# Gate and up products of a SwiGLU feed-forward as seven block products, the feed-forward in four straight-line parts with a ring of eight weight operands

## The reference

```python
D_MODEL, D_FF = 1024, 2816
def rmsnorm(x, g):
    return x * lax.rsqrt(jnp.mean(x * x, axis=-1, keepdims=True) + EPS) * g
def swiglu(h, w_gate, w_up, w_down):
    return (jax.nn.silu(h @ w_gate) * (h @ w_up)) @ w_down
def trunk(x, ...):
    for i in range(2):
        x = x + 0.5 * rmsnorm(swiglu(rmsnorm(x, ng[0]), gate[i, 0], up[i, 0], down[i, 0]), ng[1])
        h = rmsnorm(x, ng[2])
        y = pool_mixer(h) if i == 0 else gated_deltanet(h)
        x = x + rmsnorm(y, ng[3])
        x = x + 0.5 * rmsnorm(swiglu(rmsnorm(x, ng[4]), gate[i, 1], up[i, 1], down[i, 1]), ng[5])
```

## Time and profile before

| | us |
|---|---|
| median of three runs | 2585.25 |
| the profiled execution | 2587.87 |
| its span, first to last instruction | 2586.1 |
| TensorE matmul busy | 2445.6 |
| VectorE busy | 1290.9 |
| ScalarE busy | 872.7 |
| GpSimd busy | 233.9 |
| mean granted TensorE clock | 0.973 |

### The profile page before, as it was taken

One profiled execution on the slowest core, in us unless ns is written; L12 is line 12 of the kernel. 1 busy time (PEld: TensorE's weight loads), 2 busy tenths in 40 slices (PEclk: granted clock), 3 DMA queues, 4 the chain that ended last, 5 costly groups with the idle time before them and its releaser, 6 DMA issues. The chain is left out here.

```text
span 2586.1 us, 46586 instructions
## 1 busy us (share of the span) xinstructions
PE 2445.6 (95%) x18483; PEld 2352.9 (91%) x18483; DVE 1290.9 (50%) x2356; ACT 872.7 (34%) x1540; POOL 233.9 (9%) x198
## 2 busy tenths in 40 slices
PE   7999998699999999999988899999999998999997
PEld 6999998599999989999987798888987988999997
DVE  4443443754344454334435756757566446433444
ACT  4322232333122342212325546363452324322332
POOL 0000000000000000000002122142223640000000
PEclk9999999899999999999998899999999998999999
DMA  3242331022323313422312244424445342232231
GB/s 103 87 124 71 89 97 56 20 73 87 92 81 90 89 58 89 120 82 84 100 46 84 77 112 116 112 67 126 130 117 145 102 137 61 82 103 76 82 99 57
DMA packets 427016, 234.18 MB, mean 91 GB/s; under 512 B 38524, under 2 KB 417045, under 8 KB 426364
## 3 DMA queue, kind: packets, MB, share of 16 engines
q1 hardware_dynamic: 426907, 232.71, 31.3%
HBM read 205.10 MB, written 27.93 MB: 90 GB/s over the span
## 5 line engine op out<-in xcount | busy, mean ns | idle before, releaser
L887 PE MATMUL acc<-hhi,whi 128*128 128x272 f32 x2688 | 775.4, 288 | 2.6 <-DVE wlo L1908 2.6
L887 PE MATMUL acc<-hlo,whi 128*128 128x272 f32 x2688 | 776.0, 289 | 0.0
L887 PE MATMUL acc<-hhi,wlo 128*128 128x272 f32 x2688 | 773.7, 288 | 0.0
L887 PEld LDWEIGHTS acc<-hhi,whi 128*128 128x128 f32 x2688 | 506.0, 188 | 3.8 <-DVE wlo L1908 2.6
L887 PEld LDWEIGHTS acc<-hhi,wlo 128*128 128x128 f32 x2688 | 506.4, 188 | 0.0
L887 PEld LDWEIGHTS acc<-hlo,whi 128*128 128x128 f32 x2688 | 504.9, 188 | 0.0
L1908 DVE TENSOR_TENSOR wlo<-wraw,whi 128x1024 fp32r<-128x1024 f32 (+1 forms) x240 | 319.5, 1332 | 236.2 <-ACT whi L1418 236.1
L887 PE MATMUL acc<-hidhi,whi 128*128 128x272 f32 x1232 | 355.8, 289 | 5.7 <-DVE wlo L1908 5.7
L887 PE MATMUL acc<-hidhi,wlo 128*128 128x272 f32 x1232 | 357.6, 290 | 0.0
L887 PE MATMUL acc<-hidlo,whi 128*128 128x272 f32 x1232 | 355.2, 288 | 0.0
L1418 ACT ACTIVATE whi<-wraw 128x1024 fp32r<-128x1024 f32 (+1 forms) x238 | 269.5, 1133 | 253.7 <-PE acc L887 220.2
(11 more groups left out here) (296 smaller groups left out, 3144.0 us busy)
## 6 DMA issues: line engine op xcount, KB each, us to landing
wraw<-in_w_ffn_gate_dram SPq DMA_DIRECT2D x88, 512.0 KB, 3.8
wraw<-in_w_ffn_up_dram SPq DMA_DIRECT2D x88, 512.0 KB, 3.8
wraw<-in_w_ffn_down_dram SPq DMA_DIRECT2D x64, 704.0 KB, 4.6
wraw<-in_dn_w_in_dram SPq DMA_DIRECT2D x48, 512.0 KB, 4.2
room<-in_state_delta_dram SPq DMA_DIRECT2D x16, 512.0 KB, 4.7
out_delta_sample_dram<-room SPq DMA_DIRECT2D x16, 512.0 KB, 3.5
wraw<-in_dn_w_out_dram SPq DMA_DIRECT2D x16, 512.0 KB, 5.0
room<-x_blocks SPq DMA_DIRECT2D x16, 256.0 KB, 4.0
```

The lines of the kernel that those rows point to most:

```text
L887: last = pe.matmul(acc[s][0:width, hf, 0:HT], w[s][:, k, 0:width], a[:, k0 + k, cols(hf)], start=(n == 0), stop=(n == 3 * nk - 1))
```

## The change

The 22 hidden tiles of a feed-forward are now done in four parts of 2, 3, 3 and 3 pairs of tiles with no loops left: every step is written out. A step is one pair of 128-column tiles of gate or up (8 k tiles, one load of 1 MB with 256 columns), or one pair of down tiles of a part (4 or 6 k tiles).

The first part is computed as before ("plain": 2 tiles x 2 halves x 8 k x 3 matmuls). The other three use Strassen's scheme in Winograd's form: the weights of a step are a 2x2 block matrix (k halves by tiles), the activations one of k halves by column halves, and seven products of 4 k tiles take the place of eight. That needs three weight sums and one difference in place (`weight_sums`, VectorE, 128x512 each) and three activation differences (`t_h`, `t_l`, once a feed-forward). The sums of products on VectorE replace the taking out: seven additions a step, each of a PSUM bank and a tile in SBUF; the first product is copied to SBUF by ScalarE (`take_first`). Because blocks of both column halves are mixed, the activations have to be normalised first: VectorE writes x * gain * rpre into `y` (`normed`, 16 operations), from which the differences and new high and low parts are made during the first part's steps and first down steps.

Weight operands are now tiles of 4 k tiles (128x512) in a ring of eight pairs `w_h`, `w_l`, with two raw buffers of 1 MB; operand o is rounded by ScalarE as soon as product o - 8 is done. Low parts are made by GpSimd, except for the first step of a feed-forward and the operands A11 and A22 of the seven-product steps, which VectorE makes. The seven products use the eight PSUM banks in rotation. In the last part the down tiles 4 to 7 are done for half 0 and then for half 1. The pooling inputs are loaded in the last part of feed-forward 0, the zero fills are made in 16 pieces from a constant tensor during down steps of feed-forward 1, DeltaNet's small inputs are loaded behind feed-forward 2's last weights, and its buffers are laid out anew.

Core of the diff:

```diff
+FFN_CHUNKS = ((0, 2), (2, 3), (5, 3), (8, 3))
+RING = 8
+A11, S2, S3, S1, A22, S4, A12 = range(7)
...
+            def weight_sums(step):
+                raw = raws[step.raw % 2]
...
+                dve.wait_ge(raw_in[step.raw % 2], 16 * (step.raw // 2 + 1))
+                if at:
+                    dve.wait_ge(*low_ready(sevens[at - 1].op + S4))
+                a11, a21, a12 = raw[:, 0:HK4, 0, :], raw[:, 0:HK4, 1, :], raw[:, HK4:KT, 0, :]
+                dve.tensor_tensor(wsum[:, 0], a21, raw[:, HK4:KT, 1, :], ALU.add).then_inc(s_sum, 1)
+                dve.wait_ge(s_sum, step.sums + 1)
+                dve.tensor_tensor(wsum[:, 1], wsum[:, 0], a11, ALU.subtract).then_inc(s_sum, 1)
+                dve.tensor_tensor(a21, a11, a21, ALU.subtract).then_inc(s_sum, 1)
+                dve.wait_ge(s_sum, step.sums + 2)
+                dve.tensor_tensor(wsum[:, 2], a12, wsum[:, 1], ALU.subtract).then_inc(s_sum, 1)
```

GpSimd, TensorE and ScalarE in a seven-product step (`low_of` exists on VectorE too, then with `lo_dve`):

```diff
+            def low_of(step, i):
+                o = step.op + i
+                n = depth(step, i)
+                pool.wait_ge(op_hi, o + 1)
+                pool.tensor_tensor(w_l[o % RING][:, 0:n, :], source(step, i), w_h[o % RING][:, 0:n, :].bitcast(F), ALU.subtract)\
+                    .then_inc(lo_pool, 1)
...
+                for i, (h_high, h_low) in enumerate((b11, t2, t3, t1, t4, b22, b21)):
+                    b, o = product_bank(step, i), step.op + i
+                    if b in held:
+                        pe.wait_ge(*held[b])
+                    held[b] = emptied[i]
+                    pe.wait_ge(*low_ready(o))
+                    for k in range(HK4):
+                        for n, (w, h) in enumerate(((w_h, h_high), (w_l, h_high), (w_h, h_low))):
+                            last = pe.matmul(banks[b], w[o % RING][:, k, :], h[:, k, :], start=(k == 0 and n == 0),
+                                             stop=(k == HK4 - 1 and n == 2))
+                    last.then_inc(prod, 1)
...
+                    if step.kind == "gate":
+                        round_four(step, nxt)
+                        for i, s in ((4, 3), (5, 2), (6, 1)):
+                            round_op(nxt, i)
+                            silu_seven(step, s)
+                        silu_seven(step, 0)
+                    elif step.kind == "up":
+                        round_four(step, nxt)
+                        for i, (s, count) in enumerate(((3, 6), (2, 7), (1, 9), (0, 11))):
+                            if 4 + i < nxt.ops:
+                                round_op(nxt, 4 + i)
+                            hidden(step, s, count)
```

VectorE in a seven-product step:

```diff
+                    if nxt.seven:
+                        low_of(nxt, A11)
+                        weight_sums(nxt)
...
+                    dve.wait_ge(snap, step.sums // 4 + 1)
+                    add(S2, u2, p1, p6)
+                    dve.wait_ge(comb, step.comb + 1)
+                    add(S3, u3, u2, p7)
+                    dve.wait_ge(comb, step.comb + 2)
+                    add(S1, into[:, 3, :], u3, p5)
+                    add(S1, u4, u2, p5)
+                    if nxt.seven:
+                        low_of(nxt, A22)
+                    add(A22, into[:, 2, :], u3, p4)
+                    if step.kind == "up":
+                        dve.wait_ge(gate_silu, step.gates)
+                        times_silu(3, 3)
+                        times_silu(5, 2)
+                    dve.wait_ge(comb, step.comb + 4)
+                    add(S4, into[:, 1, :], u4, p3)
+                    if step.kind == "up":
+                        hidden_low(step, 0, 3)
+                        times_silu(8, 1)
+                        hidden_low(step, 1, 2)
+                    add(A12, into[:, 0, :], p1, p2)
+                    if step.kind == "up":
+                        hidden_low(step, 2, 1)
+                        times_silu(10, 0)
+                        hidden_low(step, 3, 0)
```

The first part on VectorE and GpSimd, and SP's queue:

```diff
+                for hf in range(2):
+                    dve.wait_ge(rb_ready, 4 * r + hf + 1)
+                    for m in range(2):
+                        plain_gate(steps[0], m, hf)
+                    normed(hf)
+                difference(0, b12, b11)
+                plain_up(steps[1], 0, 0)
+                difference(1, b22, tf[:, 0])
...
+                    for i in range(step.ops):
+                        if not by_vector(step, i):
+                            low_of(step, i)
+                    if step is steps[2]:
+                        low_difference(r, 0)
+                        low_difference(r, 1)
+                    if step is steps[3]:
+                        low_difference(r, 2)
...
+            def ffn(e):
+                for step in steps_of(e)[2 * (e == 1):]:
+                    load(step)
+                    if e == 0 and step is steps_of(0)[-3]:
+                        sp.wait_ge(prod, steps_of(0)[-4].op)
+                        pool_inputs()
+                    if e == 1 and step.kind == "down" and step.chunk in (1, 2):
+                        for dst in (x_blocks, u_blocks):
+                            n = 4 * step.chunk - 4 + step.p
+                            sp.dma_start(dst[16 * n:16 * (n + 1), :, :], consts[0:16, 576:704].unsqueeze(1).broadcast_to([16, 16, P]))\
+                              .then_inc(conv_in, 16)
```

## The result

| | before | changed |
|---|---|---|
| median of the runs, us | 2585.05 (4 runs) | 2488.65 (4 runs, 2487.07 to 2496.24) |
| span of the profiled execution | 2586.1 | 2485.3 |
| mean granted clock | 0.973 | 0.975 |

The ratio is 0.9635, with a 95% interval of 0.9623 to 0.9646: faster by 96 us. The forecast was 2495. The total came out as said, but two of its terms were wrong in size and one in its reason; the experiments take them apart.

What follows compares the result with a forecast made beforehand. TensorE's issue rate, 0.125 us a matmul, was taken to bound the feed-forwards. 2587.9 - 108.0 - 21.9 - 7.5 + 18 + 20 + 2 + 4 + 3 = 2497.5, less 2.6: 2495 us, range 2462 to 2565.

Steps and rivals of the forecast that it cites:

- Fewer matmuls: Gate and up steps in seven products: 84 matmuls for 96, 72 steps, 864 fewer at 0.125 us, -108.0 us.
- No loops: TensorE's 3.97 us hole after each feed-forward's last loop, with half clock behind it, goes: 4 x 5.5 = -21.9 us.
- holes remain in unrolled code: Rival: TensorE's holes stay at full count in unrolled code, +22 us, inside the range; no chance of its own.
- Zero fills: Two 1024 KB fills at 1062.6 us delay weights; as 16 pieces in another feed-forward's down steps, -7.5 us.
- Seven-product parts: VectorE's chain T, 23.8 us a pair against TensorE's 21.0, stalls each of 12 parts 1.5 us: +18 us.
- The slack: Lag of VectorE's chain that a part of three pairs and its down steps absorb: 7 us a part.
- side engines don't lead: Rival: T up to 23.3 in seven-product steps, plain part at its low end of 8 us: 2465 us, chance 0.12.
- The shared SBUF read: VectorE's two-SBUF-input operations wait for GpSimd's; at handover prices 20.5 us a pair, at whole durations 24.7, against TensorE's 21.0.
- The slower rival: VectorE waits out nearly every GpSimd operation in seven-product steps: 27.8 us a pair, 2638 us, chance 0.09.
- The point from which it decides: T = 26.3 a pair, where stalls of 9 us a part use up the 108 us left before stalls.
- The plain part: First part of each feed-forward: VectorE's normalised rows and GpSimd's low differences delay TensorE, 5 us each, +20 us (8 to 40).
- Small ones: First load of 1 MB +2, four tiles evicted in each feed-forward's last half +4, pooling input loaded late +3 us.

Runs made afterwards that it cites:

- the eighth product: Changed kernel with the last of the seven products computed twice in each of 72 steps, 864 matmuls more: 2597.7 us.
- the wait moved apart: Kernel before, TensorE waiting ahead of the halved last down pair only for its first operand's low part, for the second's behind 33 matmuls: 2561.8 us, ratio 0.9915.
- the form with T = 25.8: Changed kernel with four more VectorE additions a step, both inputs in SBUF, ahead of the weight sums where GpSimd is idle: 2584.3 us.
- the five kernels: Changed kernel, 2488.65 us; with four additions from PSUM, 2499.6; A22's low part on GpSimd, 2510.2; four from SBUF, GpSimd idle, 2584.3; four beside GpSimd, 2667.9.
- the fifth: Changed kernel with four more VectorE additions of 128x272 a seven-product step, both inputs in SBUF, beside GpSimd's work: 2667.9 us.

## Why the prediction was right and wrong

Measured terms stand beside those on record.

- *Fewer matmuls*, -108.0: measured 109.0 by the eighth product. Right.
- *No loops*, -21.9: the size was right (22 to 23 by the wait moved apart), the reason wrong. The step that failed was reading a hole without a releaser as the price of a loop's exit, and taking "it stands only there" for support. It also stood only where one wait asks for two operands. The trace of before had the row that points to it: VectorE's low part ends 0.1 us ahead of the hole's end. The rival "holes remain in unrolled code" was written against the same wrong mechanism.
- *Zero fills*, -7.5: measured 8.6. Right.
- *Seven-product parts*, +18: measured 0. The slack (7) was right, and the formula as well; the term was mis-sized by T, 23.8 forecast and 23.03 in the trace, under the threshold of 23.3 that the prediction named as its lower end. Laid by hand, both steps came out somewhat different: gate to up 9.7 for 9, up to gate 13.3 for 14.5. The rival "side engines don't lead" was true for this part.
- *The shared SBUF read.* The prices that I read from the earlier trace rows hold to 0.01 us. In the changed kernel (T = 23.03):

```profile
1019.53 1.30 POOL L886 TENSOR_TENSOR w_l<-raw,w_h 128x512 fp32r<-128x512 f32 x1
1019.98 1.40 DVE L2164 TENSOR_TENSOR w_l<-raw,w_h 128x512 fp32r<-128x512 f32 x1
1020.79 1.75 POOL L886 TENSOR_TENSOR w_l<-wsum,w_h 128x512 fp32r<-128x512 f32 x1
```

  VectorE's operation ends 0.55 us behind GpSimd's (0.30 where it has 272 columns), and GpSimd's next one 1.15 behind that; a turn of 272 and 512 columns takes 1.45 us in all, less than the two durations, 0.43 + 1.29. But these are prices of the shared read, not of VectorE's time. VectorE stands still for the rest of GpSimd's operation: in the last pair of every part (from 1006.09 to 1029.12 in the part above), 6 of its 20 operations with two SBUF inputs wait, 0.7 to 1.1 us each, 5.0 us of the 23.03. Laid by hand, a low part behind a GpSimd operation was 1.4 us (three take 1.41, 1.68 and 1.40), and four more waits were 0.5 each (there are three, of 0.75, 1.09 and 0.75). The other 14 keep their durations, because GpSimd, waiting for ScalarE's roundings, is idle over a third of these stages, and the weight sums fall into that time. So it was right not to charge whole durations to every operation, but the earlier trace rows don't tell how often VectorE waits; that came from the order of the step. The Trainium skill, "SBUF — State Buffer", section "Who interferes with whom", has an exclusive lock and the loser blocked; the trace agrees in that each operation that waits ends 0.30 or 0.55 us behind GpSimd's. The slower rival (T = 27.8, 2638 us) was thus real but 4.8 us of T away, and a form with eight more such additions a pair went past it: T = 29.2 and 2668 us. The point from which it decides, T = 26.3 on record, came out near: the form with T = 25.8 takes 2584.3 us, the kernel before beside it 2586.2.
- *The plain part*, +20 (8 to 40): 44.7 us on average for 36 of plain steps and 26.75 for 24 of first down steps, 11.5 a feed-forward above pace, 46 in all. Against the kernel before, which had small stops of its own that are gone (in each feed-forward one of 0.6 to 0.7 us early on, and in its halved last pair one of 0.9 and one of 0.4 to 1.05, some 9 us in all), the net is less: 111.0 saved inside the feed-forwards, with 108, 22 and 8.6 to be expected, leaves 27.6 lost. The causes were named rightly (up step 1.4 for 1.2; evictions 2.1 for 1; GpSimd's differences), but the differences were put at 3 us and are 4.25 with 2.4 for the clock: that one order in GpSimd's queue is 27 us.
- *Small ones*, +9: 10.3 outside the feed-forwards (0.9 at the start for 2; 4.9 at pooling for 3; 3.3 at the end, and 1.2). One cost for the last halved steps was too low: VectorE is in the residual, and its last eviction's sum lands 3.3 us late, as the wait on line 1041 shows.

So stalls in the parts, 18 too much, and the plain part, some 8 too little, cancelled in part; a total 6.4 us from the median is partly luck.

What I asked of the trace: GpSimd at 0.63 to 0.66 and VectorE at 0.91 in the seven-product windows, sums at 0.69 (they fall into GpSimd's idle time; I had expected more), low parts at 1.13, PSUM additions at 0.43. The waits on a low part or hidden low part that I expected there are absent.

## What to carry to other kernels

When a hole has no releaser in the profile, look for the operation on any other engine that ends just ahead of it before naming a cause, and read every semaphore that the waiting line asks for. A side engine that was busy 91% of a burst cost nothing here, because its lag stayed under the slack that the next stage gave back; put both in one formula and find its threshold. In a queue shared by urgent and idle work (GpSimd's first differences were ready 45 us before TensorE used them), look at the order before the durations: here one moved line gave 27 us.

## What the hardware showed that I had not expected

- VectorE with two SBUF inputs and a working GpSimd alternate operation by operation: 1432 ns an addition of 272 columns that meets a GpSimd operation, for 431 when GpSimd is idle, and 431 when one input is in PSUM whatever GpSimd does. GpSimd's operations of 512 columns then take 1.48 us instead of 1.29: the turn costs GpSimd 0.2 us and VectorE 1.0.
- A crude sum holds for four of the five kernels: VectorE's two-SBUF-input operations at their pitch (0.61 us for 512 columns, 0.35 for 272) plus GpSimd's at 1.27 give 22.8, 22.8, 24.1, 25.6 and 25.6 us a pair, where T is 23.0, 23.8, 24.2, 25.8 and 29.2. Why it holds was not tested. That the fifth fails where additions must take turns is argued from its time line, not shown by a run of its own.
- Additions with a PSUM input, put where GpSimd runs, were nearly free: 3.0 us of additions, 0.8 us of chain.
